# Moving half a unit of values ahead of the first stick-breaking scores, and the next normalised rows into the memory keys

## The reference, cut to what matters

```python
def swiglu(h, w_gate, w_up, w_down):
    return (jax.nn.silu(h @ w_gate) * (h @ w_up)) @ w_down
...
def memory_attention(mq, mem_k, mem_v):
    q = split_heads(mq)
    scores = jnp.einsum('bhsd,bhmd->bhsm', q, mem_k).astype(jnp.float32) / math.sqrt(HEAD_DIM)
    p = jax.nn.softmax(scores, axis=-1).astype(mq.dtype)
    return merge_heads(jnp.einsum('bhsm,bhmd->bhsd', p, mem_v))
...
def stick_breaking_mix(q, k, v):
    ...
        z = jnp.einsum('bhtd,bhsd->bhts', q[:, :, start:end], kb).astype(jnp.float32) * scale
        ...
        log_keep = jnp.where(before, -jax.nn.softplus(z), 0.0)
        later = lax.cumsum(log_keep, axis=3, reverse=True) - log_keep
        att = jnp.where(before, jnp.exp(jax.nn.log_sigmoid(z) + later), 0.0)
        outs.append(jnp.einsum('bhts,bhsd->bhtd', att.astype(v.dtype), vb))
...
def second_block(x, mem, ...):
    mem_kv = mem @ w_mem_kv
    mem_k = split_heads(mem_kv[..., :MEM_WIDTH])
    mem_v = split_heads(mem_kv[..., MEM_WIDTH:])
    for i in range(DEPTH_2):
        x = layer_norm(ALPHA * x + 0.5 * swiglu_2(x, ffn1_w_gate[i], ffn1_w_up[i], ffn1_w_down[i]), ...)
        ...                       # i = 0: the rwkv7 mix; i = 1: the stick-breaking mix
            proj = x @ sb_w_in[j]
            mix = stick_breaking_mix(proj[..., :c], proj[..., c:2 * c], proj[..., 2 * c:3 * c])
            mq = proj[..., 3 * c:]
        heads = jnp.concatenate([mix, memory_attention(mq, mem_k, mem_v)], axis=-1)
        ...
```

## Time and profile before

| | before |
|---|---|
| median of 3 runs | 1683.08 us (1682.01 to 1683.6) |
| the profiled execution | 1682.51 us, its span 1681.2 us |
| TensorE busy | 1635.7 us, 97% of the span |
| VectorE busy | 944.2 us, 56% |
| ScalarE busy | 789.5 us, 47% |
| GpSimd busy | 130.5 us, 8% |
| DMA | 280.67 MB, mean 167 GB/s |
| granted TensorE clock, mean | 0.983 of full |

### The profile page before, as it was taken

The page is one execution under the profiler, slowest core; times in us unless marked ns, Lnnn a source line. Parts: engine busy times, 40 slices in busy tenths (PEclk is TensorE's granted clock), DMA queues, the critical chain, the costliest instruction groups (busy, mean ns, idle before and its releaser), DMA issues. The chain is left out here.

```text
span 1681.2 us, 29818 instructions
## 1 busy us (share of the span) xinstructions
PE 1635.7 (97%) x13094; PEld 1499.5 (89%) x13094; DVE 944.2 (56%) x1199; ACT 789.5 (47%) x1047; POOL 130.5 (8%) x117
## 2 busy tenths in 40 slices
PE   7999999989999999999999999999999999999998
PEld 7999897767999989999997889999999988889997
DVE  6444463445645555455895675545745474575545
ACT  6444444434544454444665254434544454564443
POOL 0000020000000001000267101000020000001000
PEclk9999999869999999999999999999999999999999
DMA  7745453312654546555530146454655542445552
GB/s 277 273 176 188 168 176 151 126 50 88 227 199 175 187 155 213 181 193 175 180 126 4 49 178 228 176 191 161 225 176 191 186 157 100 145 175 202 195 180 75
DMA packets 40865, 280.67 MB, mean 167 GB/s; under 512 B 4794, under 2 KB 4794, under 8 KB 8864
## 3 DMA queue, kind: packets, MB, share of 16 engines
q1 hardware_dynamic: 39024, 272.40, 45.3%
q0 software_dynamic: 1712, 6.37, 1.1%
HBM read 277.14 MB, written 1.08 MB: 165 GB/s over the span
## 5 line engine op out<-in xcount | busy, mean ns | idle before, releaser
L231 PE MATMUL P<-xt,whi 128*128 128x256 f32 x5088 | 930.6, 285 | 4.6 <-ACT whi L205 1.7
L231 PEld LDWEIGHTS P<-xt,whi 128*128 128x128 f32 x5088 | 801.0, 192 | 19.1 <-issue 10.7
L231 PE MATMUL P<-xt,wlo 128*128 128x256 f32 x2544 | 701.8, 283 | 0.0
L219 DVE TENSOR_TENSOR wlo<-raw,whi 128x2048 fp32r<-128x2048 f32 x245 | 559.6, 2289 | 79.3 <-PE P L231 76.5
L205 ACT ACTIVATE whi<-raw 128x2048 fp32r<-128x2048 f32 x245 | 467.4, 1908 | 160.9 <-PE P L231 119.2
L231 PEld LDWEIGHTS P<-xt,wlo 128*128 128x128 f32 x2544 | 488.1, 192 | 0.0
L684 DVE TENSOR_TENSOR AR<-P,AR 128x256 f32<-128x256 f32 x114 | 48.3, 424 | 333.3 <-ACT AR L655 333.3
L655 ACT ACTIVATE AR<-P 128x256 f32<-128x256 f32 x114 | 43.7, 383 | 351.6 <-PE P L231 351.6
L231 PE MATMUL P<-whi,hh 128*128 128x512 f32 x504 | 197.9, 393 | 0.0
L231 PE MATMUL P<-wlo,hh 128*128 128x512 f32 x504 | 196.9, 391 | 0.0
L231 PE MATMUL P<-whi,hl 128*128 128x512 f32 x504 | 196.2, 389 | 0.0
(11 more groups left out here) (225 smaller groups left out, 924.8 us busy)
## 6 DMA issues: line engine op xcount, KB each, us to landing
raw<-ws SPq DMA_DIRECT2D x249, 1024.0 KB, 4.8
gb<-gains SPq DMA_DIRECT2D x14, 512.0 KB, 7.2
AR<-by_distance POOLq DMA_DIRECT2D x1, 3072.0 KB, 20.1
x<-x_in SPq DMA_DIRECT2D x2, 512.0 KB, 4.1
AR<-mem_in POOLq DMA_DIRECT2D x1, 1024.0 KB, 5.3
AR<-gains SPq DMA_DIRECT2D x2, 512.0 KB, 4.7
out<-x SPq DMA_DIRECT2D x2, 512.0 KB, 2.6
cs<-cst SPq DMA_DIRECT2D x1, 737.0 KB, 14.1
```

What stands on the lines that cost most here:

```text
L219: dve.e.tensor_tensor(k.wlo[n % NLO][:, :], k.raw[u % NRAW][:, :], k.whi[n % NHI][:, :].bitcast(F32), ALU.subtract).then_inc(*k.s_lo.inc(u))
L231: return pe.e.matmul(o, l, r, start=start, stop=stop, skip_group_check=True)
```

## The change

Three things move; no instruction is added or taken away.

- Stick-breaking stage: on PE the first half unit of values stands ahead of `z_tensor(0)` and the memory head 0, and `att.tensor(i)` comes after the half unit i instead of after i-1; `stick_tensor(0)` stands before the last transposes instead of after the last sums. On ACT the high part of unit U+5 is made after the third `lead_scalar` instead of after the second, and `att.scalar(4)`, which copies head 3's transposes, behind the two copies of the values (L2787) instead of ahead of them.
- Memory stage: on PE the keys are multiplied block by block (c outside, s inside) instead of tile by tile, and both transposes of FIRST stand in their middle, when the first four blocks of `xt` have been read. The wait for `MK` stands in `lead_tensor`, behind its first 16 products.
- Memory stage on ACT and DVE: the copies of FIRST stand ahead of the copy `MK` and of the high part of U_FFN3+2, the copies of SECOND ahead of that of U_FFN3+3. The low part of U_MEM+1 is made before the second half of the rows is added up, that of U_FFN3+1 after FIRST.

```diff
--- before.py
+++ after.py
@@ -464,9 +464,12 @@
     return lambda g: turn_tensor(k, pe, t, src, halves(k.s_xn, t), FIRST[g:g + 1], (4 + g,))
 
 
-def lead_tensor(k, pe, t, src, units):
+def lead_tensor(k, pe, t, src, units, need=()):
+
 
     first_tensor(k, pe, t, units[0], 0)
+    for w in need:
+        pe.wait_ge(*w)
     for h in range(2):
         pe.wait_ge(*k.s_res.after(t, 1, h))
     first_tensor(k, pe, t, units[1], 1)
@@ -1364,7 +1367,7 @@
     turn_tensor(k, pe, "mem", tiles(k.MEM), lambda a, g: [])
 
 
-def mem_tensor(k, pe):
+def mem_tensor(k, pe, lead):
     wh, wl = weights(k, U_MEM)
     pe.wait_ge(*k.s_lo.after(U_MEM))
     pe.wait_ge(*k.s_res.after("f3", 0, 1))
@@ -1376,7 +1379,19 @@
             last = mm3(pe, k.P[a][:, 0:256], k.xt[:, c, a, 0, :], k.xt[:, c, a, 1, :], wh[:, w], wl[:, w], c == 0, c == 7)
     last.then_inc(*k.s_used.inc(U_MEM))
     pe.wait_ge(*k.s_res.after("f3", 1, 0))
-    cols_tensor(k, pe, U_MEM + 1, 2)
+    wh, wl = weights(k, U_MEM + 1)
+    pe.wait_ge(*k.s_lo.after(U_MEM + 1))
+
+    for c in range(8):
+        if c == 4:
+            last.then_inc(*k.s_dn.inc("mem", "rows"))
+            for g in range(2):
+                lead(g)
+        for s in range(2):
+            w = slice((s * 8 + c) * 128, (s * 8 + c) * 128 + 128)
+            last = mm3(pe, k.P[2][:, s * NT:(s + 1) * NT], wh[:, w], wl[:, w], k.xt[:, c, :, 0, :], k.xt[:, c, :, 1, :],
+                       c == 0 and s == 0, c == 7)
+    last.then_inc(*k.s_used.inc(U_MEM + 1))
 
 
 def mem_scalar(k, act, norm):
@@ -1390,12 +1405,13 @@
     for a in range(2):
         act.wait_ge(*k.s_used.after(U_MEM))
         act.e.activation(k.MV[:, a, :], k.P[a][:, 0:256], ACT.Copy).then_inc(*k.s_ea.inc("mv", a))
+    act.wait_ge(*k.s_dn.after("mem", "rows"))
+    turn_scalar(k, act, norm.t, None, FIRST[0:1], (4,))
+    turn_scalar(k, act, norm.t, U_MEM + 1, FIRST[1:2], (5,))
+    act.e.activation(k.MK, k.P[2][:, :].rearrange("p (j m) -> p j m", j=2), ACT.Copy).then_inc(*k.s_ea.inc("mk"))
     hi_to(k, act, U_FFN3 + 2)
-    act.wait_ge(*k.s_used.after(U_MEM + 1))
-    act.e.activation(k.MK, k.P[2][:, :].rearrange("p (j m) -> p j m", j=2), ACT.Copy).then_inc(*k.s_ea.inc("mk"))
-    turn_scalar(k, act, norm.t, None, FIRST, (4, 5))
+    turn_scalar(k, act, norm.t, None, SECOND, (6, 7))
     hi_to(k, act, U_FFN3 + 3)
-    turn_scalar(k, act, norm.t, None, SECOND, (6, 7))
 
 
 def mem_vector(k, dve, norm):
@@ -1403,12 +1419,14 @@
         norm.add_vector(dve, 0, h)
     turn_vector(k, dve, "mem", QUARTERS[0:3], (4, 5, 6))
     norm.rest_vector(dve, 0)
+    lo_to(k, dve, U_MEM + 1)
     for h in range(2):
         norm.add_vector(dve, 1, h)
     turn_vector(k, dve, "mem", QUARTERS[3:4], (7,))
     norm.rest_vector(dve, 1)
+    lo_to(k, dve, U_FFN3)
+    turn_vector(k, dve, norm.t, FIRST, (4, 5))
     lo_to(k, dve, U_FFN3 + 1)
-    turn_vector(k, dve, norm.t, FIRST, (4, 5))
     turn_vector(k, dve, norm.t, SECOND, (6, 7))
 
 
@@ -2698,15 +2716,16 @@
     U = U_SB
     att, need = k.recall2, [k.s_tt.after("sb", 1, 1)]
     pe.wait_ge(*k.s_tt.after("sb", 1, 1))
-    z_tensor(k, pe, 0)
-    att.tensor(pe, 0, need)
     for i in range(4):
         values_half_tensor(k, pe, i // 2, i % 2)
-        att.tensor(pe, i + 1, need)
+        if i == 0:
+            z_tensor(k, pe, 0)
+        att.tensor(pe, i, need)
+    stick_tensor(k, pe, 0)
+    att.tensor(pe, 4, need)
     pe.wait_ge(*k.s_ea.after("vs", 0, 0))
     cols_half_tensor(k, pe, U + 5, 0, 0)
     att.tensor(pe, 5, need)
-    stick_tensor(k, pe, 0)
     cols_half_tensor(k, pe, U + 5, 0, 1)
     z_tensor(k, pe, 1)
     pe.wait_ge(*k.s_ea.after("vs", 0, 1))
@@ -2775,17 +2794,19 @@
 
     for n in range(3):
         lead_scalar(k, act, "sb", U + n, n, k.cross[n], 0.125 if n < 2 else 1.0)
-        hi_to(k, act, U + 4 + n)
+        if n != 1:
+            hi_to(k, act, U + 4 + n)
     att.scalar(act, 0)
     z_scalar(k, act, 0)
-    for i in range(1, 5):
+    for i in range(1, 4):
         att.scalar(act, i)
         if i == 2:
             hi_to(k, act, U + 7)
     for a in range(2):
         act.wait_ge(*k.s_used.after(U + 4))
         act.e.activation(k.VS[:, a, 0:512], P[a][:, :], ACT.Copy).then_inc(*k.s_ea.inc("vs", 0, a))
-    att.scalar(act, 5)
+    for i in range(4, 6):
+        att.scalar(act, i)
     stick_scalar(k, act, 0)
     hi_to(k, act, U + 8)
     head_cols_out(U + 5, 0, k.Q, 0.125, "qs", 1)
@@ -2988,12 +3009,9 @@
     mixer_tensor(k, pe, lead("f2", k.XN))
     lead_tensor(k, pe, "f2", tiles(k.XN), first_units(U_FFN2))
     ffn_tensor(k, pe, "f2", U_FFN2, None, None, lambda: mem_turn_tensor(k, pe))
-    mem_tensor(k, pe)
-    pe.wait_ge(*k.s_ea.after("mk"))
+    mem_tensor(k, pe, lead("f3", k.XN))
     pe.wait_ge(*k.s_ea.after("mv", 1))
-    for g in range(2):
-        lead("f3", k.XN)(g)
-    lead_tensor(k, pe, "f3", tiles(k.XN), first_units(U_FFN3))
+    lead_tensor(k, pe, "f3", tiles(k.XN), first_units(U_FFN3), [k.s_ea.after("mk")])
     ffn_tensor(k, pe, "f3", U_FFN3, lead("rw", k.x))
     lead_tensor(k, pe, "rw", tiles(k.x), first_units(U_RWKV))
     rwkv_inputs_tensor(k, pe)
```

## The result

| | before | after |
|---|---|---|
| median us (range, runs) | 1682.82 (1682.01 to 1683.6, 4) | 1671.05 (1669.91 to 1675.43, 4) |
| ratio, with its 95% interval | | 0.9935 (0.9916 to 0.9953) |
| profiled execution, its span | 1682.51, 1681.2 | 1669.91, 1668.6 |
| granted clock, mean | 0.983 | 0.986 |

The kernel is 11.8 us faster by the medians.

What follows compares the result with a forecast made beforehand. TensorE, busy 97% of the span, bounds the kernel, so time is won only where it idles or runs at the lower clock. 7.0 + 2.3 = 9.3 us off 1682.5 gives 1673.2, as median 1673.8; range 1672.0 to 1677.0.

Steps and rivals of the forecast that it cites:

- The stick-breaking stage: Between leading products and further queries: 3.72 us idle, 0.78 and 2.24 slow, 0.34 for copies; 7.0 us taken as won.
- Gain: 3.18 - 0.87 = 2.3 us: Memory stage: three losses of 0.64, 1.30 and 1.24 us go; 0.77 and 0.1 remain.
- The hole left: Memory stage, behind the first 8 leading products: PE still waits for the second turned group, losing 0.77 us.
- The 0.1 for switches: Memory stage: 0.1 us added to the remaining loss for PE switching between products and transposes.
- the hole of the low part: Memory stage, ahead of the keys: PE's 0.64 us wait for the low part of U_MEM+1 would go.
- The products behind them run at 5.03 us for 40, so the clock stayed up there: Memory stage: its three short holes of 0.64, 1.15 and 1.06 us were taken not to lower the clock.
- Against the profiled execution: 1682.5 - 9.3 = 1673.2: Whole kernel: 9.3 us subtracted from one execution, 0.6 us under the 1683.1 median, giving a median of 1673.8.
- The first (holes close in part): Both holes close only in part, a stick-breaking margin failing by 1 to 3 us; 1675 to 1679 us; 15%.
- both thin margins: Stick-breaking stage: first pair's keys ready 0.2 us, head 0's exponentials 0.5 us, before PE asks; no wait counted.
- The second (the low clock has another cause): Stick-breaking stage: low clock not from the hole, or a new equally long hole; 1676.8 or 1680.5 us; 5%.
- The third (DVE blocked behind POOL): Stick-breaking stage: U+5's low part starts only when POOL's first instruction ends, PE waits 0.9 us; 1674.7 us; 5%.
- The fourth (a load too late): Slower: the load of U_FFN3+4, issued 5.5 us later, lands after 637 and holds up PE's fourth gate product; 2%.

Runs made afterwards that it cites:

- Filling the hole alone: Kernel before, with 14 unused extra products put in the hole ahead of the first stick-breaking scores; 1679.53 us, ratio 0.9979.
- ACT's part: Kernel before, with only ACT's high part of U+5 moved after the third `lead_scalar`; 1680.6 us, ratio 0.9989.
- PE's part: Kernel before, with the stick-breaking stage's new product order and place of copies, but U+5's high part left where it was; 1677.36 us, ratio 0.997.
- the memory part alone: Kernel before, with only the memory-stage pieces of the change, the stick-breaking stage left as it was; 1681.6 us, ratio 0.9989.
- The low part of U_MEM+1 alone: Kernel before, with one edit: DVE makes this low part ahead of the second half of the sums; 1682.57 us, ratio 0.9998.

## Why the prediction was right or wrong

**The stick-breaking stage: right, in mechanism and size.** 7.0 forecast, 7.13 measured. Filling the hole alone shortens the stage by 3.4 us, most of it slow time given back. Leaving 2.7 us of it (ACT's part) still brings the clock down, for 3.4 us; leaving 0.66 (PE's part) doesn't. The third `lead_scalar` was reckoned at 1383.1 - 5.5 = 1377.6 and came at 1377.43, the keys at 1379.85 and came at 1380.10, the low part of U+5 ended at 1382.48 where 1382.45 was reckoned. All eight traces with both parts of this stage besides the first take 95.1 to 95.4. What is less fixed is the old stage: 102.1 to 103.0 in five traces and 100.96 in the first repeat of the kernel before, where the clock was low for a shorter time behind the same hole. So 7.1 is the usual worth, and 5.8 an occasional one.

**The memory stage: right in its mechanism, the term mis-sized.** "Gain: 3.18 - 0.87 = 2.3 us" is the step; it measured 2.83, over the upper bound of 2.7 as well. Counted from start to start, as the term was, four things were off. The hole left: the eight products from 604.95 leave off at 605.91, and the next starts at 606.52, 0.60 us instead of 0.77, because ACT began 0.19 us after 604.95 and not 0.31. The 0.1 for switches was not needed. The transposes between the keys take 0.79 (601.20 to 601.99) instead of 0.92. And the hole of the low part had been taken as its idle time, 0.64, where from start to start it is 0.80 (0.92 less the 0.12 of one product), as PE's timeline of the kernel before in its first repeat has it:

```profile
601.32 0.28 PE L231 MATMUL P<-whi,xt 128*128 128x256 f32 x1
602.24 0.47 PE L231 MATMUL P<-xt,whi 128*128 128x256 f32 x2 [0.64 <-DVE wlo L219]
```

0.17 + 0.1 + 0.13 + 0.16 = 0.56, and 0.53 was missing. One of the moves, the high parts of ACT, was neither needed nor harmful.

**The clock in the memory stage: the reading was wrong as a general one.** "The products behind them run at 5.03 us for 40, so the clock stayed up there" was read from one execution. In four of the seven traces of that stage as it was, it falls, and the stage costs 1.4 us more. The holes seem to take part in it: in the long sort it fell 4 times of 4 with the old holes, and not once in 3 traces with shorter ones. The one experiment that filled the holes for this question was caught in the short sort, so it is argued from few traces and not shown. By its own length (37.1 less 32.9) the memory part would be worth 4.2 us in the long sort. But there the clock falls later instead, 6.6 us of it in 830 to 860, in both traces with the changed stage and in none of the other five long ones. "Between the two" then takes 757.3 and 757.9 where the others take 753.4 to 756.3, about 3 us more. So in the long sort most of it is given back, and the memory part is worth some 1 to 2 us, against 2.8 in the short one. The times of the runs fit: 1.9 us for the memory part alone, with 0 to 3.9 as its interval. Two traces are few for this, and why the clock falls at 832 was not tried.

**The range: here the prediction failed.** Its bounds for the two terms, 6.0 to 7.2 and 1.5 to 2.7, add up to medians of 1673.2 to 1675.6; the range went 1.2 us below that, with no working for it. And the step that failed is the sum itself: "Against the profiled execution: 1682.5 - 9.3 = 1673.2. That execution lies 0.6 us under the median". That takes the untouched stretches ahead of the two stages and between them, some 1340 us, as fixed: their scatter was put at nothing, and no reason was given. They aren't fixed. In the profiled pair they give 2.7 us, and for the 1.85 ahead of the memory stage a cause can be seen. The windows of 296 to 302, before and then after:

```profile
296.00:302.00 6.00, 5.59 (x21) 4.26 (x21) 2.57 (x10) 2.89 (x6) 0.00 (x0) 0.72 0.79 330
```

```profile
296.00:302.00 6.00, 5.60 (x27) 4.40 (x27) 2.57 (x10) 2.51 (x6) 0.00 (x0) 1.00 0.79 329
```

The first execution had 3.4 us at the lower level there (6 x 0.28 / 0.5), which costs 1.7 us, and the second none; nothing of the change acts at 300 us. The 14 runs of the changed kernel lie in two groups, nine in 1669.9 to 1672.2 and five in 1674.9 to 1676.8, with a median of 1671.7 and a mean of 1672.7. The profiled ones of the lower group are all of the short sort, the one of the upper group of the long sort. The 78 runs of the kernel before spread from 1676.5 to 1687.8. The three runs shown beforehand happened to lie within 1.6 us of each other, and three of the first four of the changed kernel in its lower group. Of the miss against 1673.8, 2.75 us, 0.1 is the stick-breaking term, 0.5 the memory term, and the rest scatter of the untouched part. So the miss is in the main bad luck with the first four runs, on a range that had no room for it: 1683.1 less the 10.0 us of the two stages is 1673.1, inside the range. Because the times lie in two groups, a median of few runs jumps with the group that holds more of them; that of all 14 still lies 0.3 us below the range, their mean inside it. Over six more runs of the changed kernel, beside 28 of the kernel before, the gain was 9.6 us (0.9943), where 9.3 had been summed; from the mean of all 78 runs of the kernel before on record (1683.0) to that of the 14 it is 10.3.

**The rivals.** The first (holes close in part) did not happen: both thin margins held in every trace of the changed kernel, by 0.1 to 0.6 us. The second (the low clock has another cause) falls with the filled hole. The third (DVE blocked behind POOL) falls with the rows at 1380.15 and 1377.48: inside POOL's instruction DVE took 2.33 us, where alone it takes 2.2 to 2.3. The Trainium skill, page "SBUF — State Buffer", section "Who interferes with whom", would have it start only when POOL ends, here near 1382.1; this trace doesn't agree. It may be POOL that is held up: its instruction with the low part inside took 4.59 us and the next one 3.07. But the kernel's work on POOL differs in length in other places too (2.77 to 4.59 us in this trace), and no run tells what sets it. The fourth (a load too late) did not happen: from 607 to 650 PE waits for nothing.

## What to carry to other kernels

Where the matrix engine is the bound, look at the granted clock behind a long hole, and where it falls charge the hole twice, as idle time and as slow time. Test the second half by filling the hole with spare products. Here 3.7 us of lost starts carried 3 more, and a hole of 2.7 us still brought the clock down, while single ones of 0.46 and 0.66 us did not. A granted clock that is read from one execution is a reading and no constant; where several short holes stand close together, look at two or three executions before you build on it. The range of a forecast needs the scatter of the untouched rest as well as the margins of the change, and three runs that agree don't measure it.

## What the runs showed of the hardware that was not expected

- Three holes of 0.64, 1.15 and 1.06 us within 10 us stood ahead of 3.4 us of low clock in 4 of 7 executions, and always in those in which it had been low longer in the mixer 220 us earlier. Whether the two have a common cause stays open.
- Behind the same hole of 3.6 us the low clock lasts 6.8 us in most executions and 3.4 in one.
- Where a slow stretch is removed, another can turn up elsewhere: 6.6 us at 830 to 860, in both long executions with the new memory stage, though not in the long one of "The low part of U_MEM+1 alone", whose memory stage kept its clock too.
